# The diagonal block of a bidirectional state-space mixer: both directions in one exponential, step sizes applied by GpSimd to the mask product, one matmul per head

## The chip, the cores and the metric

The kernel runs on one core of a Trainium2 chip. The metric is the device time of one execution in microseconds. The engines are TensorE (PE; its weight loads are listed as PEld), VectorE (DVE), ScalarE (ACT), GpSimd (POOL) and SyncE (SP), each with its own instruction queue; they meet through semaphores.

## What is computed

The layer is an encoder: RMSNorm with modulation, an input projection, two mixers side by side (8 heads of latent attention, 8 heads of a bidirectional Mamba-2 scan), an output projection, then a 16-expert mixture and a last RMSNorm. It runs on a prompt of 512 tokens and a sample of 1024. The change concerns the part of the scan within a chunk of 128 tokens:

```python
cs = jnp.cumsum(dt * a.reshape(g, r), axis=2)
seg = cs[:, :, :, None] - cs[:, :, None, :]
decay_in = jnp.exp(jnp.where(lower, seg, -jnp.inf))
cb = jnp.einsum('bcqgn,bcsgn->bcqsg', cm, bm)
m = cb[..., None] * decay_in * dt[:, :, None]
y_diag = jnp.einsum('bcqsgr,bcsgrp->bcqgrp', m, x)
...
y_fwd = _ssd_scan(xh, dt[:, :, 0], a[0], bm, cm)
y_bwd = flip(_ssd_scan(flip(xh), flip(dt[:, :, 1]), a[1], flip(bm), flip(cm)))
y = y_fwd + y_bwd + d_skip.astype(f32)[:, None] * xh.astype(f32)
```

So for each head there is a 128x128 decay matrix for the forward direction (target at or after source) and one for the backward direction (target at or before source), each times a group's C·B product and a source's step size dt, and both are multiplied with the same x.

## The kernel before, in words

The 1,536 tokens are 12 tiles of 128: tiles 0 to 3 are the prompt, tiles 4 to 11 the sample. The program runs in stages (`inputs`, `attend`, `output`, `choice`, `experts`, `final`). The change is in `attend`, in the function `mixers`, which runs once for the prompt and once for the sample. In it each engine has a body for one tile g that goes through the 8 attention heads h = 0 to 7 (512 keys for the prompt, 1024 for the sample), and work of the scan, of the previous tile's end and of the next tile's query (`front`) is written by hand between the heads. The order on an engine is the order in the code; nothing is scheduled.

For a head, PE makes the scores (L1792) one head ahead, DVE takes their row maximum (`tops`, L1586) and turns it into a bias (L1589), ACT takes the exponential (L1475), PE turns the result in two halves (`turn_p`, L1805), ACT copies the first half (L1536) and DVE the second (L1715), and every second head PE multiplies with the values (L1815). PE's scores two heads on wait for DVE's copy.

The scan's diagonal part of a tile before the change:

- DVE, head 2 of the tile before: `steps` splits the step terms into a high and a low part (L1597, L1599). DVE (`terms`, L1604; head 3 and head 7) and POOL (`terms`, L1424) multiply them with a triangle of ones, DVE for the forward direction and POOL for the backward one: `r_sum`.
- PE (`seg`, L1843) multiplies `r_sum` with a strict triangle, which gives the segment sums of four heads of one direction in bank `b_y`: four rounds p = 0 to 3 (direction and group), two matmuls each, at heads 0 and 1.
- ACT (`seg_exp`, L1501) takes the exponential of each round, 128x512. PE's next round waits for it.
- DVE (`masked`, L1615) multiplies C·B with the two masks, and (`weights`, L1626) each of the four exponentials with that.
- POOL (L1434) makes `xdt`, x times the step sizes for both directions, in one 128x1024 product. It waits until the tile before has used its own.
- PE (`diag`, L1882) multiplies per head and direction: 16 products of 128x128 with 128x64, summed in pairs in `b_y`. It waits for DVE's `take_off` (L1631), and comes at the end of head 3.

DVE also rotates the next tile's query in head 3 (`rope`, L1135 to L1140, six products), for which PE waits at head 4 (`front`, L1782), and normalises the attention output in head 4 (`norm_o`, L1668), ahead of the maximum of head 5. POOL's third product, D times x (L1439), waits for `gate` (L1650) of the tile before. DVE's `add_off` (L1638), `add_skip` (L1643) and `gate` assemble y at heads 4 and 5.

```python
wait_apart(pool, steps_done, g + 1, pool_turns)
wait_apart(pool, seg_mm, g * 4, pool_turns)
```

These two waits open POOL's `terms`; `wait_apart` is a wait on POOL's own queue.

## Time and profile before

| | us |
|---|---|
| median of 3 runs | 3012.91 (3012.7 to 3015.11) |
| the profiled execution, span from first to last instruction | 3010.1 |
| that execution with what lies around the span (by the median of the runs) | 3012.9 |
| the stage with both mixers, from the prompt's first scores to the last tile's end | 362 to 911 |
| one prompt tile in the middle | 32.6 |
| one sample tile in the middle | 45.3 |

The profiled execution has no separate total of its own beside its span; the runs lie about 2.8 us above that span. The rows are of this one execution. In the timeline a line is: start, duration, engine, line of the kernel, operation, output<-input, shape, count, and in brackets how long the engine sat idle before it and what released it.

### The profile page before, as it was taken

To read this page: it belongs to the slowest core of one execution; us is meant where nothing else is said; L and a number is where in the kernel's file an instruction comes from. 1 tells how busy PE (TensorE), PEld (TensorE's weight loads), DVE (VectorE), ACT (ScalarE), POOL (GpSimd) and SP (SyncE) were. 2 spreads that over 40 slices of the span, in tenths; PEclk is the share of its full clock that TensorE was granted. 3 is DMA by queue.
4 is the path that set the end of the run, shared out by engine and by line. 5 is a ranking of instruction groups with operands and counts; after the bars stand their busy time and mean duration, and the time that the engine had idled before them with its cause. 6 is when DMAs were issued, how large, how long until landed. Compare 5 with 4: busy or idle time off the path is not lost. (4 is left out here: it accounts for less than half of the span.)

```text
span 3010.1 us, 50890 instructions
## 1 busy us (share of the span) xinstructions
PE 2784.9 (93%) x17878; PEld 2411.1 (80%) x17878; DVE 2161.3 (72%) x4155; ACT 1529.6 (51%) x2880; POOL 200.8 (7%) x192
## 2 busy tenths in 40 slices
PE   5999688999998966999999999999999999999993
PEld 4999465666666856999999999999999999999992
DVE  3565776666664458788788788778778778778774
ACT  4443454544543324555555555555555556556552
POOL 0000121011100001000000000000000000000001
PEclk8999898999999978999999999999999999999996
DMA  6111310212214336677677677677677777777654
GB/s 258 63 66 57 118 37 30 94 51 101 99 42 177 140 139 210 219 248 252 218 246 248 223 244 243 226 244 242 228 247 238 228 250 239 227 251 239 228 186 178
DMA packets 359719, 547.41 MB, mean 182 GB/s; under 512 B 14784, under 2 KB 287936, under 8 KB 359616
## 3 DMA queue, kind: packets, MB, share of 16 engines
q1 hardware_dynamic: 350720, 514.59, 50.0%
q0 software_dynamic: 8896, 31.46, 4.5%
q8 instruction: 63, 1.03, 0.1%
q14 instruction: 40, 0.33, 0.0%
HBM read 493.51 MB, written 52.49 MB: 181 GB/s over the span
## 5 line engine op out<-in xcount | busy, mean ns | idle before, releaser
L2606 PE MATMUL banks<-rowsT_parts,weights_high 128*128 128x384 f32 x4096 | 1183.9, 361 | 11.0 <-DVE hidden_parts L2535 7.2
L2607 PE MATMUL banks<-rowsT_parts,weights_low 128*128 128x192 f32 x4096 | 1026.0, 250 | 0.0
L2606 PEld LDWEIGHTS banks<-rowsT_parts,weights_high 128*128 128x128 f32 x4096 | 769.7, 188 | 19.9 <-DVE hidden_parts L2535 9.9
L2607 PEld LDWEIGHTS banks<-rowsT_parts,weights_low 128*128 128x128 f32 x4096 | 783.1, 191 | 1.4
L2472 DVE TENSOR_TENSOR weights_low<-keys_or_w_out,weights_high 128x1024 fp32r<-128x1024 f32 x512 | 603.2, 1217 | 1.4 <-ACT weights_high L2412 1.4
L2412 ACT ACTIVATE weights_high<-keys_or_w_out 128x1024 fp32r<-128x1024 f32 x512 | 523.9, 1049 | 39.6 <-PEq L2210 39.6
L2617 PE MATMUL banks<-weights_high,hidden_parts 128*128 128x512 f32 x1536 | 435.7, 392 | 0.0
L2522 DVE TENSOR_TENSOR h_or_keys_or_sums<-banks,h_or_keys_or_sums 128x192 f32<-128x192 f32 x512 | 181.4, 354 | 327.7 <-ACT h_or_keys_or_sums L2438 327.7
L2438 ACT ACTIVATE h_or_keys_or_sums<-banks 128x192 f32<-128x192 f32 x512 | 165.6, 324 | 457.5 <-PE banks L2607 453.5
L2617 PEld LDWEIGHTS banks<-weights_high,hidden_parts 128*128 128x128 f32 x1536 | 283.4, 188 | 69.8
L2617 PE MATMUL banks<-weights_low,hidden_parts 128*128 128x512 f32 (+1 forms) x1024 | 319.4, 393 | 0.0
L2472 DVE TENSOR_TENSOR weights_low<-slab_down,weights_high 128x1024 fp32r<-128x1024 f32 x256 | 311.4, 1216 | 0.0
L2412 ACT ACTIVATE weights_high<-slab_down 128x1024 fp32r<-128x1024 f32 x256 | 264.3, 1051 | 5.3 <-PE banks L2617 4.9
L2617 PEld LDWEIGHTS banks<-weights_low,hidden_parts 128*128 128x128 f32 (+1 forms) x1024 | 164.9, 161 | 55.8
L2446 ACT ACTIVATE silu_gate<-h_or_keys_or_sums 128x192 f32<-128x192 f32 x256 | 92.5, 361 | 228.3 <-DVE h_or_keys_or_sums L2522 228.3
L1792 PE MATMUL banks<-keys_or_w_out,arena_attend 96*128 96x512 f32 x320 | 159.2, 606 | 6.2 <-DVE arena_attend L1715 4.3
L2385 POOL DMA_INDIRECT residual<-weighted,rows_out x32 | 49.8, 1556 | 1675.5 <-DVE weighted L2511 1675.5
L1536 ACT ACTIVATE arena_attend<-banks 128x512 f32<-128x512 f32 (+1 forms) x96 | 50.5, 526 | 187.8 <-PE banks L1805 187.7
L1586 DVE TENSOR_REDUCE mix_top<-banks 128x1 f32<-128x1024 f32 (+1 forms) x96 | 100.1, 1043 | 42.4 <-PE banks L1792 42.1
L2163 PE MATMUL banks<-w_out_high,mixed_parts 128*128 128x512 f32 x384 | 125.2, 397 | 2.1 <-DVE mixed_parts L2126 1.6
L1805 PEld LDWEIGHTS banks<-masks,arena_attend 128*128 128x128 f32 x640 | 75.6, 142 | 56.2 <-issue 31.9
L995 PE MATMUL banks<-w_in_high,h_parts 128*128 128x512 f32 (+1 forms) x384 | 116.5, 380 | 0.0
(303 smaller groups left out, 3528.7 us busy)
## 6 DMA issues: line engine op xcount, KB each, us to landing
keys_or_w_out<-w_gate SPq DMA_DIRECT2D x128, 1024.0 KB, 5.1
keys_or_w_out<-w_up SPq DMA_DIRECT2D x128, 1024.0 KB, 6.8
slab_down<-w_down SPq DMA_DIRECT2D x128, 1024.0 KB, 4.8
arena_attend<-w_ada SPq DMA_DIRECT2D x8, 2048.0 KB, 7.6
arena_attend<-ssd_tiles SPq DMA_DIRECT2D x12, 992.0 KB, 9.0
arena_inputs<-w_ada SPq DMA_DIRECT2D x4, 2048.0 KB, 11.4
ssd_tiles<-arena_inputs SPq DMA_DIRECT2D x24, 256.0 KB, 2.0
mixed<-arena_attend SPq DMA_DIRECT2D x12, 512.0 KB, 3.3
```

The costliest lines, as they stand in the source:

```text
L995: mm = nc.tensor.matmul(out, a, b, start=(k == 0 and n == 0), stop=(k == KD - 1 and n == 2))
L1586: nc.vector.tensor_reduce(top[:, h % 2:h % 2 + 1], core.banks[:, h % 2 * 1024:h % 2 * 1024 + keys_n], AX_X, ALU.max).then_inc(topped, 1)
L1792: mm = nc.tensor.matmul(core.banks[:, h % 2 * 1024 + k0:h % 2 * 1024 + k0 + 512], qT[j][0:DQK, h, :], kT[0:DQK, h, k0:k0 + 512], start=Tru ...
L2163: mm = nc.tensor.matmul(core.ps[6 * j + half], a, b[:, k, cols], start=(k + n == 0), stop=(k == 7 and n == 2))
L2412: nc.scalar.activation(like(n, w_hi), unit_of(raw, n), ACT.Copy).then_inc(unit_hi, 1)
L2438: nc.scalar.activation(sums[:, kind, fc % 2], core.ps[2 * (fc % 2) + kind][:, CT:2 * CT], ACT.Copy).then_inc(low_out, 1)
L2446: nc.scalar.activation(sil[:, fc % 2], sums[:, 0, fc % 2], ACT.Silu).then_inc(sil_done, 1)
L2472: nc.vector.tensor_tensor(like(n, w_lo), unit_of(raw, n), like(n, w_hi[:].bitcast(F32)), ALU.subtract).then_inc(unit_lo, 1)
L2522: nc.vector.tensor_tensor(sums[:, kind, fc % 2], core.ps[2 * (fc % 2) + kind][:, 0:CT], sums[:, kind, fc % 2], ALU.add).then_inc(sum_done, 1)
L2606: nc.tensor.matmul(out[:, 0:2 * CT], w_hi[:, u, block], x[:, k, :], start=k == 0, stop=False)
L2607: mm = nc.tensor.matmul(out[:, 0:CT], w_lo[:, u, block], x[:, k, 0:CT], start=False, stop=k == KD - 1)
L2617: mm = nc.tensor.matmul(y_banks[b][0:rows, cols], h_parts[:, fc, tokens], w[:, u, cols], start=step == 0 and first, stop=step == STEPS - 1 ...
```

## The change

Since a strict triangle gives zero outside its direction's half, the segment sums of both directions can be added into one bank: each of the two rounds now has four matmuls (two directions, two parts) and gives four heads of both directions. One exponential per round follows, so two of 128x512 per tile in place of four. The masks move into a new product of POOL, `cb_times_dt`: mask times step sizes for each direction (two of 128x1024), their sum (128x1024), and that times C·B (two of 128x512). DVE multiplies the two exponentials with it (`weights`), and `masked` keeps only its two copies. `diag` is one product per head on x itself: 8 in place of 16. POOL's `xdt` is gone. The tile `cbdt` takes the room of `e`'s second half, and `xdt` and `cbm` are no longer there.

```diff
             def terms(g, j):
...
-                wait_apart(pool, seg_mm, g * 4, pool_turns)
+                wait_apart(pool, seg_mm, g * 2, pool_turns)
...
+            def cb_times_dt(g, j):
+
+                wait_apart(pool, m_done, g * 2, pool_turns)
+                for d, (out, m) in enumerate(((cbdt, M_LE), (cbdt_b, M_GE))):
+                    nc.gpsimd.tensor_tensor(out, core.masks[:, m, :].unsqueeze(1).broadcast_to([P, NS, P]),
+                                            dt[j][:, 8 * d:8 * d + 8].unsqueeze(2).broadcast_to([P, NS, P]),
+                                            ALU.mult).then_inc(cbdt_order, 1)
+                wait_apart(pool, cbdt_order, g * 3 + 2, pool_turns)
+                nc.gpsimd.tensor_tensor(cbdt, cbdt, cbdt_b, ALU.add).then_inc(cbdt_order, 1)
+                wait_apart(pool, cbdt_order, g * 3 + 3, pool_turns)
+                for grp in range(2):
+                    part = cbdt[:, 4 * grp:4 * grp + 4, :]
+                    ins = nc.gpsimd.tensor_tensor(part, part, cb[j][:, P * grp:P * grp + P].unsqueeze(1).broadcast_to([P, 4, P]),
+                                                  ALU.mult)
+                ins.then_inc(cbdt_done, 1)
...
             def first():
                 if not r:
                     terms(lo, 0)
+                    cb_times_dt(lo, 0)
...
-                wait_apart(pool, diag_mm, g, pool_turns)
-                nc.gpsimd.tensor_tensor(xdt, heads(xnat[j]).unsqueeze(1).broadcast_to([P, 2, NS, HP]),
...
                 if after(i, more)[0]:
                     terms(g + 1, 1 - j)
+                    cb_times_dt(g + 1, 1 - j)
...
-            def seg_exp(g, p):
+            def seg_exp(g, grp):
...
-                nc.scalar.activation(e[:, p // 2, 4 * (p % 2):4 * (p % 2) + 4, :], b_y.rearrange("p (h q) -> p h q", h=4),
+                nc.scalar.activation(e[:, 4 * grp:4 * grp + 4, :], b_y.rearrange("p (h q) -> p h q", h=4),
...
-                for d in range(2):
-                    nc.vector.tensor_tensor(cbm[:, d], cb[j].rearrange("p (a q) -> p a q", a=2),
...
+            def weights(g, grp):
+
+                if grp == 0:
+                    dve.wait_ge(cbdt_done, g + 1)
+                dve.wait_ge(e_done, g * 2 + (grp + 1))
+                part = e[:, 4 * grp:4 * grp + 4, :]
+                nc.vector.tensor_tensor(part, part, cbdt[:, 4 * grp:4 * grp + 4, :], ALU.mult).then_inc(m_done, 1)
...
                     if h in (1, 2):
-                        weights(g, 2 * h - 2)
+                        weights(g, h - 1)
...
-                    if h in (1, 2):
-                        weights(g, 2 * h - 1)
...
+                for d in range(2):
+                    for part in range(2):
+                        mm = nc.tensor.matmul(b_y, turns_r[:, d, :],
+                                              r_sum[:, part, d, 4 * grp:4 * grp + 4, :].rearrange("p h q -> p (h q)"),
+                                              start=d + part == 0, stop=d + part == 2)
...
                 for h in range(NS):
-                    for d in range(2):
-                        mm = nc.tensor.matmul(b_y[:, h * HP:(h + 1) * HP], e[:, d, h, :], xdt[:, d, h, :],
-                                              start=(d == 0), stop=(d == 1))
+                    mm = nc.tensor.matmul(b_y[:, h * HP:(h + 1) * HP], e[:, h, :], xnat[j][:, h * HP:(h + 1) * HP],
+                                          start=True, stop=True)
```

The order on the engines moves at three places. The first is POOL, one tile, around one tile's `terms` (L1424; L1434 is `xdt`, L1439 D times x). Before:

```order
L1434 TENSOR_TENSOR arena_attend<-arena_attend 128x1024
L1439 TENSOR_TENSOR arena_attend<-arena_attend,rows 128x512
L1424 TENSOR_TENSOR decay_steps<-masks,steps_high 128x1024
L1424 TENSOR_TENSOR decay_steps<-masks,steps_low 128x1024
L1434 TENSOR_TENSOR arena_attend<-arena_attend 128x1024
```

With the change (L1423 is `terms`; L1431, L1435 and L1439 are `cb_times_dt`; L1450 is D times x):

```order
L1450 TENSOR_TENSOR arena_attend<-arena_attend,rows 128x512
L1423 TENSOR_TENSOR decay_steps<-masks,steps_high 128x1024
L1423 TENSOR_TENSOR decay_steps<-masks,steps_low 128x1024
L1431 TENSOR_TENSOR arena_attend<-masks,arena_attend 128x1024 x2
L1435 TENSOR_TENSOR arena_attend<-arena_attend 128x1024
L1439 TENSOR_TENSOR arena_attend<-arena_attend 128x512 x2
```

POOL's block behind `terms` has five instructions where it had one, and they stand in the same run as `terms`, where `xdt` came after the wait for `diag`.

The second is DVE, prompt tile 0, head 2 into head 3: the second copy of `turn_p`, the scan's steps, and the maximum of head 4. Before:

```order
L1586 TENSOR_REDUCE mix_top<-banks 128x1
L1589 TENSOR_SCALAR mix_bias<-mix_top 128x1
L1715 COPY arena_attend<-banks 128x256
L1626 TENSOR_TENSOR arena_attend<-arena_attend 128x512
L1597 CAST steps_high<-arena_attend 128x16
L1599 TENSOR_TENSOR steps_low<-arena_attend,steps_high 128x16
L1631 TENSOR_TENSOR arena_attend<-banks,arena_attend 128x512
L1586 TENSOR_REDUCE mix_top<-banks 128x1
```

With the change:

```order
L1596 TENSOR_REDUCE mix_top<-banks 128x1
L1599 TENSOR_SCALAR mix_bias<-mix_top 128x1
L1719 COPY arena_attend<-banks 128x256
L1607 CAST steps_high<-arena_attend 128x16
L1609 TENSOR_TENSOR steps_low<-arena_attend,steps_high 128x16
L1635 TENSOR_TENSOR arena_attend<-banks,arena_attend 128x512
L1596 TENSOR_REDUCE mix_top<-banks 128x1
```

The product `weights` (L1626 before) between the copy and `steps` (L1597, now L1607) is gone, so `steps`, which POOL waits for, comes one product earlier.

The third is PE, prompt tile 0, from the state's first product (L1858, now L1861) to the values of head 4. Before:

```order
L1858 MATMUL banks<-arena_attend,c_groups 128x256 x2
L1792 MATMUL banks<-keys_or_w_out,arena_attend 128x512
L1805 MATMUL banks<-masks,arena_attend 128x128 x2
L1858 MATMUL banks<-arena_attend,c_groups 128x256 x2
L1805 MATMUL banks<-masks,arena_attend 128x128 x2
L1882 MATMUL banks<-arena_attend 128x64 x16
L1792 MATMUL banks<-keys_or_w_out,arena_attend 128x512
L1815 MATMUL banks<-arena_attend 64x128 x8
```

With the change:

```order
L1861 MATMUL banks<-arena_attend,c_groups 128x256 x2
L1794 MATMUL banks<-keys_or_w_out,arena_attend 128x512
L1807 MATMUL banks<-masks,arena_attend 128x128 x2
L1861 MATMUL banks<-arena_attend,c_groups 128x256 x2
L1807 MATMUL banks<-masks,arena_attend 128x128 x2
L1883 MATMUL banks<-arena_attend 128x64 x8
L1794 MATMUL banks<-keys_or_w_out,arena_attend 128x512
L1817 MATMUL banks<-arena_attend 64x128 x8
```

Nothing moves here but the count of the diagonal's products: 16 before, 8 now, at the same place.

## Rows read from the trace of the kernel before

**Rows 1.** The page, busy time of each engine: us (share of the span) xinstructions

```profile
PE 2784.9 (93%) x17878; PEld 2411.1 (80%) x17878; DVE 2161.3 (72%) x4155; ACT 1529.6 (51%) x2880; POOL 200.8 (7%) x192
```

**Rows 2.** Windows of one tile each: PE, PEld, DVE, ACT, POOL busy (x), PEclk, DMA

```profile
402.70:435.30 32.60, 29.23 (x191) 20.51 (x190) 26.37 (x56) 16.57 (x47) 6.73 (x4) 0.96 0.01 5
635.80:681.10 45.30, 44.12 (x369) 31.15 (x368) 31.15 (x58) 22.09 (x50) 6.70 (x4) 1.00 0.22 83
```

**Rows 3.** Timeline, PE, sample tile: start us, us, engine line op, names, shapes [idle before]

```profile
656.76 3.76 PE L1882 MATMUL banks<-arena_attend 128*128 128x64 f32 x32 [0.45 <-DVE arena_attend L1631]
660.35 1.94 PE L1792 MATMUL banks<-keys_or_w_out,arena_attend 96*128 96x512 f32 x4
```

**Rows 4.** Lines, ACT exponentials and DVE weights: duration ns min/median/max

```profile
L1501 ACT ACTIVATE arena_attend<-banks x48: 587/597/626, 371.6 to 872.0; 128x512 f32<-128x512 f32 x48
L1626 DVE TENSOR_TENSOR arena_attend<-arena_attend x48: 679/682/685, 373.0 to 877.1; 128x512 f32<-128x512 f32 x48
```

**Rows 5.** Timeline, POOL, same sample tile

```profile
653.95 1.90 POOL L1424 TENSOR_TENSOR decay_steps<-masks,steps_high 128x1024 fp32r<-128x1024 f32 x1 [25.88 <-DVE steps_low L1599]
655.81 1.90 POOL L1424 TENSOR_TENSOR decay_steps<-masks,steps_low 128x1024 fp32r<-128x1024 f32 x1
660.70 1.90 POOL L1434 TENSOR_TENSOR arena_attend<-arena_attend 128x1024 f32<-128x1024 f32 x1 [2.99 <-PE banks L1882]
```

**Rows 6.** Timeline, DVE and POOL, first prompt tile

```profile
362.37 1.23 DVE L1604 TENSOR_TENSOR decay_steps<-masks,steps_high 128x1024 fp32r<-128x1024 f32 x1
362.71 2.65 POOL L1424 TENSOR_TENSOR decay_steps<-masks,steps_high 128x1024 fp32r<-128x1024 f32 x1 [362.12 <-DVE steps_low L1599]
363.52 2.92 DVE L1604 TENSOR_TENSOR decay_steps<-masks,steps_low 128x1024 fp32r<-128x1024 f32 x1
365.32 2.87 POOL L1424 TENSOR_TENSOR decay_steps<-masks,steps_low 128x1024 fp32r<-128x1024 f32 x1
366.36 1.98 DVE L1570 TENSOR_SCALAR arena_attend<-h_or_keys_or_sums,mix_q_rstd 128x256 f32<-128x256 f32 x1
368.15 1.94 POOL L1434 TENSOR_TENSOR arena_attend<-arena_attend 128x1024 f32<-128x1024 f32 x1
370.06 1.04 POOL L1439 TENSOR_TENSOR arena_attend<-arena_attend,rows 128x512 f32<-128x512 f32 x1
```

**Rows 7.** Timeline, DVE, same sample tile, heads 3 and 4

```profile
655.93 0.68 DVE L1631 TENSOR_TENSOR arena_attend<-banks,arena_attend 128x512 f32<-128x512 f32 x1
657.13 0.73 DVE L1135 TENSOR_TENSOR arena_attend<-arena_attend,rope 128x128 f32<-128x128 f32 x1
658.91 1.22 DVE L1604 TENSOR_TENSOR decay_steps<-masks,steps_high 128x1024 fp32r<-128x1024 f32 x1
660.04 0.48 DVE L1668 TENSOR_SCALAR arena_attend<-arena_attend,mix_o_rstd 128x512 f32<-128x512 f32 x1
662.32 1.23 DVE L1586 TENSOR_REDUCE mix_top<-banks 128x1 f32<-128x1024 f32 x1 [1.80 <-PE banks L1792]
```

**Rows 8.** Timeline, DVE and PE, same sample tile, what follows

```profile
664.61 0.60 PE L1782 MATMUL banks<-masks,arena_attend 128*96 128x128 f32 x4
668.21 1.22 DVE L1586 TENSOR_REDUCE mix_top<-banks 128x1 f32<-128x1024 f32 x1
669.56 0.69 DVE L1715 COPY arena_attend<-banks 128x512 f32<-128x512 f32 x1
670.30 1.13 PE L1792 MATMUL banks<-keys_or_w_out,arena_attend 96*128 96x512 f32 x2 [0.58 <-DVE arena_attend L1715]
```

**Rows 9.** Timeline, DVE, first prompt tile, heads 3 to 5

```profile
385.17 1.74 DVE L1135 TENSOR_TENSOR arena_attend<-arena_attend,rope 128x128 f32<-128x128 f32 x1
389.77 0.69 DVE L1586 TENSOR_REDUCE mix_top<-banks 128x1 f32<-128x512 f32 x1 [0.60 <-PE banks L1792]
394.08 0.68 DVE L1586 TENSOR_REDUCE mix_top<-banks 128x1 f32<-128x512 f32 x1
```

**Rows 10.** Timeline, DVE, first prompt tile, first weights product

```profile
373.01 0.68 DVE L1626 TENSOR_TENSOR arena_attend<-arena_attend 128x512 f32<-128x512 f32 x1
```

More of the change, by code:

```diff
@@ L1127 @@
 A_QT, A_O = 28800, 30848
-A_E, A_XDT, A_Y, A_CBM = 32896, 34944, 35968, 38016
+A_E, A_CBDT, A_Y = 32896, 33920, 35968
 A_REC, A_JUNKM = 38528, 24064
@@ L1291, in mixers @@
     step_lo = core.once("steps_low", [P, 2, 16])
-    e = A.at(A_E, 2, NS, P)
-    xdt = A.at(A_XDT, 2, NS, HP)
+    e = A.at(A_E, NS, P)
+    cbdt, cbdt_b = A.at(A_CBDT, NS, P), A.at(A_CBDT + 1024, NS, P)
     y = A.at(A_Y, 4, DSSD)
-    cbm = A.at(A_CBM, 2, 2, P)
     ctz = core.once("c_groups", [P, 2, P])
@@ L1311, in mixers @@
     act_order, o_order, rope_order, inv_done = sem("q_act_order"), sem("att_o_order"), sem("att_rope_order"), sem("att_inv")
-    terms_f, terms_b, seg_mm, e_done, m_done, cbm_done, ctz_done, xdt_done, xd_done = (
-        sem(n) for n in ("terms_f", "terms_b", "seg_mm", "seg_exp", "m_done", "cbm_done", "c_groups", "xdt_done", "xd_done"))
+    terms_f, terms_b, seg_mm, e_done, m_done, cbdt_done, ctz_done, cbdt_order, xd_done = (
+        sem(n) for n in ("terms_f", "terms_b", "seg_mm", "seg_exp", "m_done", "cb_dt", "c_groups", "cb_dt_order", "xd_done"))
     off_mm, off_done, diag_mm, y_order, gated, y_sq, s_rstd_done, y_normed, y_turned, y_mixed = (
@@ L1539, in body @@
                     if h < 2:
-                        seg_exp(g, 2 * h)
+                        seg_exp(g, h)
                     if h + 1 < NH:
@@ L1613, in masked @@
                 nc.vector.tensor_copy(ctz[64:128, 1, :], ct[j][64:128, :]).then_inc(ctz_done, 1)
-                for d in range(2):
-                    nc.vector.tensor_tensor(cbm[:, d], cb[j].rearrange("p (a q) -> p a q", a=2),
-                                            core.masks[:, (M_LE, M_GE)[d], :].unsqueeze(1).broadcast_to([P, 2, P]),
-                                            ALU.mult).then_inc(cbm_done, 1)
-            def weights(g, p):
-                d, grp = divmod(p, 2)
-                if p == 0:
-                    dve.wait_ge(cbm_done, g * 2 + 2)
-                dve.wait_ge(e_done, g * 4 + (p + 1))
-                part = e[:, d, 4 * grp:4 * grp + 4, :]
-                nc.vector.tensor_tensor(part, part, cbm[:, d, grp:grp + 1, :].broadcast_to([P, 4, P]),
-                                        ALU.mult).then_inc(m_done, 1)
+            def weights(g, grp):
+                if grp == 0:
+                    dve.wait_ge(cbdt_done, g + 1)
+                dve.wait_ge(e_done, g * 2 + (grp + 1))
+                part = e[:, 4 * grp:4 * grp + 4, :]
+                nc.vector.tensor_tensor(part, part, cbdt[:, 4 * grp:4 * grp + 4, :], ALU.mult).then_inc(m_done, 1)
             def take_off(g, j, d):
@@ L1696, in body @@
                     if h == 0:
-                        masked(g, j)
+                        c_groups(g, j)
                     if before and h == 1:
@@ L1832, in turn_o, with seg @@
                 mm.then_inc(o_turned, 1)
-            def seg(g, p, behind):
-                d, grp = divmod(p, 2)
-                pe.wait_ge((terms_f, terms_b)[d], g + 1 if d else g * 2 + 2)
-                if p:
-                    pe.wait_ge(e_done, g * 4 + p)
+            def seg(g, grp, behind):
+                pe.wait_ge(terms_f, g * 2 + 2)
+                pe.wait_ge(terms_b, g + 1)
+                if grp:
+                    pe.wait_ge(e_done, g * 2 + 1)
                 elif behind is not None:
                     pe.wait_ge(y_mixed, behind + 1)
-                for part in range(2):
-                    mm = nc.tensor.matmul(b_y, turns_r[:, d, :],
-                                          r_sum[:, part, d, 4 * grp:4 * grp + 4, :].rearrange("p h q -> p (h q)"),
-                                          start=part == 0, stop=part == 1)
+                for d in range(2):
[3 more added lines that the diff above has]
+                                              start=d + part == 0, stop=d + part == 2)
                 mm.then_inc(seg_mm, 1)
@@ L1850, in off @@
                 if d == 0:
-                    pe.wait_ge(e_done, g * 4 + 4)
+                    pe.wait_ge(e_done, g * 2 + 2)
                     pe.wait_ge(ctz_done, g + 1)
@@ L1918, in body @@
                     if h < 2:
-                        seg(g, 2 * h, g - 1 if before or r else None)
+                        seg(g, h, g - 1 if before or r else None)
                     if h == 3:
@@ L1931, in body @@
                     if h == 3:
-                        diag(g)
+                        diag(g, j)
                     if before and h == 6:
```

18 lines of the change are left out of this document (5 added, 13 removed).

## The prediction

> **What bounds the kernel now.** I read the page's busy times first [rows 1]: PE 93%, DVE 72%, POOL 7% over the whole span. These are averages over stages, and the change touches one of them, so the next view was the windows of single tiles in that stage [rows 2]. A sample tile lasts 45.3 us, with PE busy 44.1 of them, DVE 31.2 and POOL 6.7: there PE is the bound. A prompt tile lasts 32.6 us, with PE at 29.2 and DVE at 26.4: there neither is full, and the time is a chain that goes scores, maximum, exponential, turn, copy from engine to engine. The chain that ended last lies wholly in the final stage and says nothing of this one. So for each part I ask two things: what it takes off PE in a sample tile, and what it does to the time at which DVE delivers the maximum of a head, on which both kinds of tile hang. The third view was the timeline of one sample tile and of the first prompt tile. A measurement of this kernel can tell about 0.2%, some 6 us, from no change.
>
> **PE.** The diagonal's 16 products are 32 passes, and the next matmul starts 3.6 us after the first of them (656.76 to 660.35) [rows 3]. Half of them gone is 1.8 us per tile if PE is the bound, 21.6 us over 12 tiles. The segment sums keep their eight matmuls, and only stand in two runs of four. The first exponential waits for two matmuls more, the second comes later than the second did; I take that at nothing, since ACT is idle for half of a sample tile [rows 2]. If ACT were full it would cost the two matmuls, under 1 us.
>
> **ACT and DVE, work removed.** ACT loses two exponentials of 0.60 us and DVE two products of 0.68 us [rows 4], and DVE also loses the two mask products, which are half as wide. That is 1.2 us on ACT and about 2 us on DVE per tile, all at heads 0 to 2. In a sample tile PE covers them (DVE has 14 us free), so nothing. In a prompt tile the exponential of the next head stands behind the scan's on ACT, so a little may come through: between 0 and 2 us, and I take 0.5 us, because one of the two exponentials that stay now waits for its later matmuls.
>
> **POOL.** It loses `xdt`, 1.9 us, and gains three products of 128x1024 and two of 128x512. The nearest rows for these are 1.90 us for L1424 and 1.04 us for the 128x512 product at 370.06 [rows 5, 6]. Laid end to end, started every 1.86 us as the first two are, that is about 7.7 us, so POOL goes from 6.7 to 12.6 us of a 45.3 us tile. The result is needed only at head 1 of the next tile, over 10 us after it is done. By busy time this is free, and in the steady tiles no wait on the result itself will show.
>
> **Where it is not free.** The timeline of the first prompt tile has DVE and POOL side by side [rows 6]. A DVE product of 1.22 us starts at 362.37; POOL's, issued at 362.71, takes 2.65 us, that is 1.90 after the DVE product has ended. The DVE product at 363.52 takes 2.92: it ends 1.1 us after POOL's first has ended at 365.36. POOL's second (365.32) takes 2.87 and ends 1.9 us after that. The DVE scaling at 366.36 takes 1.98 us and ends 0.15 us after POOL is done. So of these instructions only one runs at a time, and at each release the one that has waited goes, so they take turns. Not every DVE instruction is concerned: at 655.93 one that reads PSUM and SBUF runs in its usual 0.68 us in the middle of POOL's second product, while the first rotation product at 657.13 takes 0.73 us and ends just after that product (657.71) [rows 5, 7]. In the prompt the same one takes 1.74 us [rows 9].
>
> The change puts five more POOL instructions exactly there. `steps` comes 0.6 us earlier (one DVE product less ahead of it), so POOL's `terms` run from 653.3 to 657.1 and `cb_times_dt` follows at once, where before POOL was silent from 657.7 to 660.7 [rows 5]. DVE then has eight instructions of the kind that waits: six rotation products, its own `terms` and `norm_o`, which took from 657.71 to 660.52 together, 2.8 us [rows 7]. If each POOL instruction gets its turn among the eight, DVE is through at 657.1 + 7.7 + 2.8 = 667.6 us. POOL waits for its own results twice inside the block, and in such a gap a DVE instruction may slip in; then up to two of the five fall behind DVE's eight, and it is through at 665.6. I take the middle, 666.6.
>
> Queued behind these on DVE is the maximum of head 5, which started at 662.32 after 1.80 us of idling for PE [rows 7]. It starts 4.3 us later. From it to the maximum of head 6, without waiting, are 1.35 us (the maximum and its bias) and the 2.5 us of the four instructions between 665.68 and 668.21: 3.9 us, so 670.5 in place of 668.21; the copy of head 5 follows 1.35 us later, and 0.74 us after its start PE can begin the second half of scores 7 [rows 8]. That is 672.6 in place of 670.30: **a sample tile gets 2.3 us longer** (1.3 to 3.3), and PE's 1.8 us are lost in this wait, since the diagonal lies ahead of it. PE will also stand at the turn of the rotated query (664.61 before [rows 8]). Seven sample tiles have a next one: 7 x 2.3 = 16 us. The last has none, and keeps its 1.8 us.
>
> In a prompt tile POOL's `terms` end at 386.2, and DVE is through at 386.2 + 7.7 + 2.4 = 396.3, or 2 earlier; middle 395.3. The maximum of head 5 was at 389.77 and that of head 6 at 394.08 [rows 9], 3.1 us behind it when DVE does not wait: 398.4, 4.3 us later. Less the 0.5 us above and rounded, **a prompt tile gets 4 us longer** (3 to 5): 16 us over four.
>
> At the very start POOL's block stands before the first tile's `weights`. POOL is done with `terms` at 368.2, and with the block near 376.2, where `weights` ran at 373.01 [rows 10]: 3.2 us late, of which DVE's waiting for PE hides a part; I take 2 (1 to 3.2).
>
> The Trainium skill (SBUF — State Buffer, the section on the two separate sides) calls the pair of ports that DVE and GpSimd share an exclusive lock, held for a whole instruction, against DVE instructions with two SBUF inputs or in a 2-port mode. It does not say who is next when it comes free. If DVE kept it over its eight instructions it would wait once, 1.9 us, be through at 657.1 + 1.9 + 2.8 = 661.8, before the maximum can start, and the sum would be the gain of rival one below; rows 6 show turns instead.
>
> **Sum.** 16 + 16 + 2 - 1.8 = 32 us on the profiled span of 3010.1 us, plus the 2.8 us by which the median of the runs (3012.9) lies above it: 3045 us. With the terms' lower bounds it is 20 us (3033), with the upper ones 45 us (3058).
>
> **Rivals.** One: the DVE instructions get through (they wait once, or PE's slack at heads 4 to 6 covers them), and the removed matmuls count. For it: DVE is idle 14 us of a sample tile, and 1.8 us of that stands right before the maximum of head 5. Then 1.8 us x 8 in the sample, and 0 to 1.8 x 4 in the prompt: 14 to 22 us faster, 2991 to 2999 us. It decides if DVE's eight instructions are delayed by less than about 1.8 us; the four alternations of rows 6 speak against it. Two: half of the turns slip by, and wait and gain cancel: 3007 to 3019. Three: the waits also lower the clock. The granted clock was 1.00 in the sample tile and 0.96 in the prompt one, where PE is less busy [rows 2], so new idle stretches may send a part of each tile to the lower of the two levels (1.2 of 2.4 GHz). At 0.96 in the sample's seven tiles, some 4% of 45.3 us each, that is 12 us more: 3057 or above.
>
> **How the numbers follow.** The forecast has 0.62, rival three 0.14, both slower; rival two 0.06, no change; rival one 0.18, faster. The time is that of the forecast, 3045. The range goes from 3004 to 3066: it leaves out rival one (0.18) and little above. The forecast's own range is 3033 to 3058.
>
> **What would show it.** Right: the six rotation products and DVE's `terms`, 2.9 us busy in a sample tile without waiting, together take over 5 us longer; POOL's five products directly behind `terms`; PE idle at heads 4 to 6 for DVE's maximum, copy or rotation, while its diagonal takes 1.8 us; sample tiles of 47 to 49 us, prompt tiles of 35.5 to 37.5. Wrong: sample tiles of 43.5 us with rotation products of 0.28 us, or a loss at heads 0 to 2, which this text takes as nothing.

## The result and the profile after

The changed kernel takes 3063.1 us (median of 4 runs, 3058.81 to 3063.99) against 3013.1 us, a ratio of 1.016 (95% interval 1.0148 to 1.0172): 50 us slower, where 32 were forecast. Its profiled execution has a span of 3062.2 us, 52.1 more than before, and a time of 3063.9 us.

The page's busy times of the kernel after, which answer to [rows 1]:

```profile
PE 2791.5 (91%) x17686; PEld 2403.2 (78%) x17686; DVE 2214.4 (72%) x4107; ACT 1518.2 (50%) x2856; POOL 287.0 (9%) x240
```

PE has 192 passes fewer (96 products of the diagonal, two passes each), and POOL is busy for 287 us in place of 201. Windows of one prompt tile and two sample tiles of the kernel after (busy of PE, PEld, DVE, ACT, POOL; granted clock of TensorE; DMA share; GB/s), against [rows 2]:

```profile
421.40:458.70 37.30, 29.88 (x175) 19.72 (x174) 30.35 (x53) 16.08 (x48) 14.47 (x8) 0.86 0.13 46
677.90:729.10 51.20, 46.62 (x352) 31.34 (x351) 36.53 (x55) 21.30 (x48) 13.63 (x8) 0.90 0.20 75
829.20:878.00 48.80, 44.32 (x352) 30.17 (x351) 36.27 (x55) 21.30 (x48) 13.65 (x9) 0.97 0.20 75
```

A sample tile takes 48.8 or 51.2 us where it took 45.3, a prompt tile 37.3 where it took 32.6. POOL is busy for 13.6 us of a sample tile where 12.6 were forecast: its sum of two whole tensors (L1435) takes 2.35 to 2.39 us in each of the twelve tiles, where I had put the 1.90 of L1424, and a product with C·B (L1439) at least 1.26 us, where I had put 1.04. It is not DVE that makes them that long; rows of e2 below show it. DVE is busy for 36.5 or 36.3 us, five more than before, though it has fewer instructions: it is booked as busy while it waits for POOL. The granted clock is 0.97 and 0.90 where it was 1.00.

Where the 52 us lie, by marks that both timelines have (the first product of POOL's `terms` for a tile, the first matmul of a stage):

| stretch | before, us | after, us | difference |
|---|---|---|---|
| start to tile 0's `terms` | 362.7 | 364.8 | 2.0 |
| to tile 1's | 20.3 | 21.0 | 0.7 |
| to tile 4's (three prompt tiles) | 100.7 | 110.5 | 9.8 |
| to tile 5's (last of the prompt, sample keys) | 79.9 | 82.6 | 2.7 |
| to tile 11's (six sample tiles) | 271.5 | 299.2 | 27.7 |
| to the output projection | 91.9 | 93.5 | 1.6 |
| to the experts | 232.9 | 233.1 | 0.2 |
| experts, first to last gate product | 1785.9 | 1792.6 | 6.7 |
| the rest | 64.3 | 65.0 | 0.7 |

The mixers hold 42.5 us, and 6.7 lie in the expert stage, of which no line was changed. Start and rest scatter by about as much between the kernels below.

The cause in a sample tile, first on DVE and POOL. Timeline of the kernel after, DVE, heads 3 and 4 of the tile at 678 (compare [rows 7]; L1596 is the maximum of head 5):

```profile
681.68 1.98 DVE L1135 TENSOR_TENSOR arena_attend<-arena_attend,rope 128x128 f32<-128x128 f32 x1
683.58 1.98 DVE L1136 TENSOR_TENSOR arena_attend<-arena_attend,rope 128x128 f32<-128x128 f32 x1
685.49 0.28 DVE L1137 TENSOR_TENSOR arena_attend<-arena_attend,rope 128x128 f32<-128x128 f32 x1
685.69 2.44 DVE L1138 TENSOR_TENSOR arena_attend<-arena_attend,rope 128x128 f32<-128x128 f32 x1
688.16 0.29 DVE L1139 TENSOR_TENSOR arena_attend<-arena_attend 128x128 f32<-128x128 f32 x1
688.37 1.35 DVE L1140 TENSOR_TENSOR arena_attend<-arena_attend 128x128 f32<-128x128 f32 x1
689.64 2.29 DVE L1614 TENSOR_TENSOR decay_steps<-masks,steps_high 128x1024 fp32r<-128x1024 f32 x1
691.85 0.47 DVE L1672 TENSOR_SCALAR arena_attend<-arena_attend,mix_o_rstd 128x512 f32<-128x512 f32 x1
692.25 1.21 DVE L1596 TENSOR_REDUCE mix_top<-banks 128x1 f32<-128x1024 f32 x1
```

And POOL in the same stretch (compare [rows 5]):

```profile
679.76 1.90 POOL L1423 TENSOR_TENSOR decay_steps<-masks,steps_low 128x1024 fp32r<-128x1024 f32 x1
681.62 3.80 POOL L1431 TENSOR_TENSOR arena_attend<-masks,arena_attend 128x1024 f32<-128x1024 f32 x2
685.59 2.38 POOL L1435 TENSOR_TENSOR arena_attend<-arena_attend 128x1024 f32<-128x1024 f32 x1 [0.18 <-POOL arena_attend L1431]
688.15 2.69 POOL L1439 TENSOR_TENSOR arena_attend<-arena_attend 128x512 f32<-128x512 f32 x2 [0.18 <-POOL arena_attend L1435]
```

The first rotation product waits for POOL's first mask product (to 683.5), the second for the next (to 685.4), the third slips into the 0.18 us in which POOL waits for its own result, the fourth waits for the sum, the fifth slips in again, the sixth waits for one product with C·B, and DVE's `terms` for the last. The eight instructions last from 681.68 to 692.3 in place of 657.13 to 660.5. The maximum behind them takes 1.21 us as ever, but POOL is done by then (690.84); that a maximum, which reads PSUM, is not slowed beside a POOL product is shown by e1 below.

Then on PE, the same stretch (compare [rows 3, 8]; L1883 is the diagonal, L1784 the turn of the rotated query, L1794 the scores):

```profile
681.31 1.97 PE L1883 MATMUL banks<-arena_attend 128*128 128x64 f32 x16 [0.45 <-DVE arena_attend L1635]
683.12 1.94 PE L1794 MATMUL banks<-keys_or_w_out,arena_attend 96*128 96x512 f32 x4
689.77 0.64 PE L1784 MATMUL banks<-masks,arena_attend 128*96 128x128 f32 x4 [2.24 <-DVE arena_attend L1140]
694.34 2.07 PE L1794 MATMUL banks<-keys_or_w_out,arena_attend 96*128 96x512 f32 x2 [1.74 <-DVE arena_attend L1719]
696.21 1.06 PE L1807 MATMUL banks<-masks,arena_attend 128*128 128x128 f32 x4
```

The diagonal takes 1.8 us in place of 3.6 (683.12 less 681.31). After it PE stands 2.24 us for the sixth rotation product and 1.74 us for DVE's copy of head 4, which is queued behind the maximum of head 5. The last row shows a third loss: four turn passes (x4) take 1.06 us where the same four take 0.60 elsewhere in the tile, so PE runs at the lower of its two clock levels (1.2 of 2.4 GHz). It does so from about 690.7, between the two waits, to 700.9, some 10 of the tile's 51.2 us, which is what the window's 0.90 says.

### The profile page after: what moved, and what is told of

Same layout as the page of the kernel before. It is cut to its first block and busy times, and to the rows that moved or that the text cites. A ratio compares the mean times of both kernels' runs of the same rounds, so it can differ in the third digit from the quotient of the medians.

```text
span 3062.2 us, 50465 instructions
## 1 busy us (share of the span) xinstructions
PE 2791.5 (91%) x17686; PEld 2403.2 (78%) x17686; DVE 2214.4 (72%) x4107; ACT 1518.2 (50%) x2856; POOL 287.0 (9%) x240
## 5 line engine op out<-in xcount | busy, mean ns | idle before, releaser
L2445 ACT ACTIVATE silu_gate<-h_or_keys_or_sums 128x192 f32<-128x192 f32 x256 | 92.6, 362 | 232.9 <-DVE h_or_keys_or_sums L2521 232.9
L1794 PE MATMUL banks<-keys_or_w_out,arena_attend 96*128 96x512 f32 x320 | 176.6, 662 | 14.9 <-DVE arena_attend L1719 13.0
L1487 ACT ACTIVATE arena_attend<-banks,mix_bias 128x1024 f32<-128x1024 f32 (+1 forms) x96 | 93.1, 970 | 93.7 <-DVE mix_bias L1599 93.6
L1596 DVE TENSOR_REDUCE mix_top<-banks 128x1 f32<-128x1024 f32 (+1 forms) x96 | 100.2, 1043 | 33.9 <-PE banks L1794 33.3
```

The source lines that it names most:

```text
L1487: nc.scalar.activation(prob[h % 2][:, 0:keys_n], core.banks[:, h % 2 * 1024:h % 2 * 1024 + keys_n], ACT.Exp, bias=bias[:, h % 2:h % 2 + 1] ...
L1596: nc.vector.tensor_reduce(top[:, h % 2:h % 2 + 1], core.banks[:, h % 2 * 1024:h % 2 * 1024 + keys_n], AX_X, ALU.max).then_inc(topped, 1)
L1794: mm = nc.tensor.matmul(core.banks[:, h % 2 * 1024 + k0:h % 2 * 1024 + k0 + 512], qT[j][0:DQK, h, :], kT[0:DQK, h, k0:k0 + 512], start=Tru ...
L2445: nc.scalar.activation(sil[:, fc % 2], sums[:, 0, fc % 2], ACT.Silu).then_inc(sil_done, 1)
```

## Experiments

The two theories: DVE and GpSimd take turns at something that both need, so five long POOL instructions behind `terms` hold up DVE's eight and through them PE; or the new order at heads 0 to 2 (a run of four matmuls, two exponentials, the wait for POOL's product) costs the time. In the table a ratio is to the kernel before on the same chip; "tile" is the distance of two tiles' `terms` in the profiled execution, in the prompt between tiles 2 and 3 and in the sample between tiles 8 and 9.

| kernel | median us | ratio (95%) | prompt tile | sample tile | experts |
|---|---|---|---|---|---|
| before | 3013.1 | | 32.6 | 45.3 | 1785.9 |
| the change | 3063.1 | 1.0160 (1.0148 to 1.0172) | 37.3 | 51.2 | 1792.6 |
| e1 block moved | 3007.6 | 0.9985 (0.9976 to 0.9995) | 33.7 | 43.7 | 1792.1 |
| e2 block small | 2995.5 | 0.9945 (0.9926 to 0.9965) | 29.7 | 43.7 | 1792.1 |
| e3 block in 16 | 3027.3 | 1.0042 (1.0026 to 1.0059) | 34.5 | 45.3 | 1792.3 |
| e4 before plus block | 3053.8 | 1.0131 (1.0114 to 1.0148) | 39.7 | 47.9 | 1786.0 |
| e5 change, diagonal twice | 3061.9 | 1.0157 (1.0141 to 1.0172) | 36.9 | 48.9 | 1792.3 |
| e6 moved, diagonal twice | 3031.4 | 1.0058 (1.0043 to 1.0074) | 35.5 | 45.5 | 1792.5 |
| e7 moved, padded | 3003.5 | 0.9967 (0.9955 to 0.9979) | 33.7 | 43.7 | 1786.7 |
| e8 moved, padded, in 16 | 2997.7 | 0.9946 (0.9932 to 0.9960) | 31.7 | 43.7 | 1786.3 |
| e9 before, padded by 3 | 3013.9 | 0.9999 (0.9990 to 1.0007) | 32.6 | 45.3 | 1785.9 |
| e10 change, padded | 3058.2 | 1.0143 (1.0128 to 1.0158) | 37.3 | 48.8 | 1786.6 |
| e11 as e8, tile 0 in long products | 2994.8 | 0.9934 (0.9921 to 0.9946) | 31.7 | 43.7 | 1786.1 |

The change's six sample tiles are 49.5, 49.7, 51.2, 51.2, 48.9 and 48.8 us; e10's, which has the same mixers, lie between 48.5 and 50.7, and e3's between 44.9 and 46.9. The longest tiles of each are those with its lowest granted clock (0.90 in the change and e10, 0.96 in e3).

**e1: the block at another place.**

```diff
             def first():
                 if not r:
                     terms(lo, 0)
-                    cb_times_dt(lo, 0)
...
                 wait_apart(pool, gated, g, pool_turns)
+                cb_times_dt(g, j)
...
                     terms(g + 1, 1 - j)
-                    cb_times_dt(g + 1, 1 - j)
```

> The change with cb_times_dt taken from behind terms to the wait for the tile before's gate (head 5), ahead of D times x; nothing else differs. Turn-taking theory: at heads 6 and 7 DVE has fewer instructions of the kind that waits (gate, norm_y, terms' second part, two copies) and more room, so rope products fall back to 0.3 to 0.7 us, PE keeps its 1.8 us per sample tile, the clock is 1.00 there: sample tiles of 43.5 to 45 us, 2992 to 3010 us in all. Rival, that the new order at heads 0 to 2 (four matmuls in a run, two exponentials, the wait for POOL's product) costs the time: stays at 3055 to 3065.

Measured: 3007.6 us. Everything that the change does is still done, and only the place of POOL's block differs, so the new order at heads 0 to 2 is not what costs. Windows of this kernel, one prompt and one sample tile:

```profile
418.70:452.40 33.70, 28.19 (x175) 18.44 (x174) 28.23 (x53) 16.37 (x48) 14.28 (x9) 0.95 0.15 51
697.50:741.20 43.70, 42.51 (x352) 29.29 (x351) 30.95 (x55) 21.21 (x48) 14.48 (x8) 1.00 0.23 87
```

The sample tile is 1.6 us shorter than before the change and PE is busy for all but 1.2 us of it; the clock is 1.00 again. The prompt tile is still 1.1 us longer than before. Its timeline shows why: at the new place DVE's second part of `terms` and its two copies wait. DVE, e1:

```profile
470.08 3.04 DVE L1613 TENSOR_TENSOR decay_steps<-masks,steps_low 128x1024 fp32r<-128x1024 f32 x1
474.31 1.31 DVE L1621 COPY c_groups<-arena_attend 64x128 f32<-64x128 f32 x1
475.63 0.99 DVE L1622 COPY c_groups<-arena_attend 64x128 f32<-64x128 f32 x1
```

They take 1.22, 0.21 and 0.22 us without company. The maximum does not wait. DVE and POOL of e1, in a sample tile:

```profile
718.94 1.22 DVE L1595 TENSOR_REDUCE mix_top<-banks 128x1 f32<-128x1024 f32 x1 [1.47 <-PE banks L1793]
718.83 2.36 POOL L1435 TENSOR_TENSOR arena_attend<-arena_attend 128x1024 f32<-128x1024 f32 x1 [0.18 <-POOL arena_attend L1431]
```

**e2: the block small.**

```diff
-            def cb_times_dt(g, j):
+            def cb_times_dt(g, j, n=8):
...
-                    nc.gpsimd.tensor_tensor(out, core.masks[:, m, :].unsqueeze(1).broadcast_to([P, NS, P]),
+                    nc.gpsimd.tensor_tensor(out[:, :, 0:n], core.masks[:, m, 0:n].unsqueeze(1).broadcast_to([P, NS, n]),
```

> The change with cb_times_dt in full for tile 0 only; from tile 1 its five instructions at the same place cover 8 of 128 columns each (the other columns keep tile 0's values: the mask product of all later tiles is left out but for these). Turn-taking theory: the five hold the ports for some 0.1 to 0.2 us each, rope is as before, 2990 to 3003 us. Rival, heads 0 to 2: 3055 to 3065. Rival, that the number of POOL instructions counts and not their length: over 3040.

Measured: 2995.5 us. The number of POOL instructions and all waits are those of the change, only their length is gone, and with it 68 us. This is also what the rest of the change is worth: its windows

```profile
414.05:443.73 29.68, 26.39 (x175) 17.64 (x174) 23.13 (x53) 16.18 (x48) 7.22 (x8) 1.00 0.16 57
681.10:724.80 43.70, 42.51 (x352) 29.29 (x351) 29.28 (x55) 21.19 (x48) 6.36 (x8) 1.00 0.24 87
```

have 43.7 us for a sample tile and 29.7 for a prompt tile, 2.9 less than before. I had expected half a microsecond from the lighter heads 0 to 2 and nothing from the diagonal; the 2.9 us hold both, and the runs do not part them here (the diagonal's part is 1.8 us in e6 against e1). With 6.2 us in the expert stage taken off, an estimate from the table, it would be at 2989.

In e2's first tile, where the block is in full, DVE reads PSUM or has one short instruction beside the sum, and stands idle beside the two products with C·B. POOL, e2:

```profile
372.82 2.35 POOL L1435 TENSOR_TENSOR arena_attend<-arena_attend 128x1024 f32<-128x1024 f32 x1 [0.18 <-POOL arena_attend L1431]
375.35 2.52 POOL L1439 TENSOR_TENSOR arena_attend<-arena_attend 128x512 f32<-128x512 f32 x2 [0.18 <-POOL arena_attend L1435]
```

So 2.35 and 1.26 us are what these instructions take by themselves.

**e3: the same work in shorter instructions.**

```diff
-                    nc.gpsimd.tensor_tensor(out, core.masks[:, m, :].unsqueeze(1).broadcast_to([P, NS, P]),
-                                            dt[j][:, 8 * d:8 * d + 8].unsqueeze(2).broadcast_to([P, NS, P]),
-                                            ALU.mult).then_inc(cbdt_order, 1)
+                    for q in range(0, NS, 2):
+                        ins = nc.gpsimd.tensor_tensor(out[:, q:q + 2, :], core.masks[:, m, :].unsqueeze(1).broadcast_to([P, 2, P]),
+                                                      dt[j][:, 8 * d + q:8 * d + q + 2].unsqueeze(2).broadcast_to([P, 2, P]),
+                                                      ALU.mult)
```

(and so for the sum and the products with C·B)

> The change with the same products at the same place, in 16 POOL instructions of 128x256 instead of three of 128x1024 and two of 128x512. By the two shapes seen (1.04 and 1.90 us) one should take 0.6 us, the block 9.8 us in place of 7.7. Turn-taking theory: each of DVE's eight instructions waits for one of 0.6 us, under 5 us in place of 7.7, so sample tiles of 46 to 48 us and prompt tiles shorter by 2 to 3 us: 3025 to 3045 us. Rival, that DVE loses what POOL works in all, whoever's turn it is: 2 us more per tile than the change, 3075 to 3090.

Measured: 3027.3 us, 36 us less than the change, at the same place and with more work on POOL. The rows are the plainest of the study. DVE, e3:

```profile
758.90 0.69 DVE L1135 TENSOR_TENSOR arena_attend<-arena_attend,rope 128x128 f32<-128x128 f32 x1
759.52 0.70 DVE L1136 TENSOR_TENSOR arena_attend<-arena_attend,rope 128x128 f32<-128x128 f32 x1
760.14 0.70 DVE L1137 TENSOR_TENSOR arena_attend<-arena_attend,rope 128x128 f32<-128x128 f32 x1
760.75 0.70 DVE L1138 TENSOR_TENSOR arena_attend<-arena_attend,rope 128x128 f32<-128x128 f32 x1
761.49 0.59 DVE L1139 TENSOR_TENSOR arena_attend<-arena_attend 128x128 f32<-128x128 f32 x1
762.00 0.69 DVE L1140 TENSOR_TENSOR arena_attend<-arena_attend 128x128 f32<-128x128 f32 x1
762.62 1.63 DVE L1618 TENSOR_TENSOR decay_steps<-masks,steps_high 128x1024 fp32r<-128x1024 f32 x1
764.17 0.84 DVE L1676 TENSOR_SCALAR arena_attend<-arena_attend,mix_o_rstd 128x512 f32<-128x512 f32 x1
```

POOL, e3:

```profile
758.83 5.89 POOL L1432 TENSOR_TENSOR arena_attend<-masks,arena_attend 128x256 f32<-128x256 f32 x8
764.90 3.26 POOL L1438 TENSOR_TENSOR arena_attend<-arena_attend 128x256 f32<-128x256 f32 x4 [0.18 <-POOL arena_attend L1432]
```

Each rotation product takes 0.6 to 0.7 us in place of 0.28: each waits for exactly one POOL product of 128x256. POOL's eight products take 5.89 us, 0.74 each, since it waits for DVE's as well. That is turns, one instruction each; a loss in proportion to POOL's work would have made this kernel the slowest.

**e4: the block alone, in the kernel before.** It writes to room that nothing reads, and POOL waits for itself four times in it where the change's block waits twice, because both mask products share that room.

```diff
+            def block(g, j):
+                order = xdt_done
+                wait_apart(pool, order, g * 5 - 4, pool_turns)
+                for d, m in enumerate((M_LE, M_GE)):
+                    if d:
+                        wait_apart(pool, order, g * 5 - 3, pool_turns)
+                    nc.gpsimd.tensor_tensor(spare, core.masks[:, m, :].unsqueeze(1).broadcast_to([P, NS, P]),
...
                 if after(i, more)[0]:
                     terms(g + 1, 1 - j)
+                    block(g + 1, 1 - j)
```

> The kernel before, with a block of five POOL products of the same shapes as cb_times_dt behind terms, written to room that nothing reads (one more wait of POOL on itself than in the change); nothing is removed. Turn-taking theory: the waits come without any of the change's other parts: sample tiles of 49 to 52 us, 3055 to 3080 us. Rival, heads 0 to 2 of the change: no effect, 3012 to 3018.

Measured: 3053.8 us, 41 us over before, by the block alone. DVE, e4:

```profile
684.89 1.98 DVE L1136 TENSOR_TENSOR arena_attend<-arena_attend,rope 128x128 f32<-128x128 f32 x1
687.00 1.98 DVE L1138 TENSOR_TENSOR arena_attend<-arena_attend,rope 128x128 f32<-128x128 f32 x1
689.22 1.98 DVE L1140 TENSOR_TENSOR arena_attend<-arena_attend 128x128 f32<-128x128 f32 x1
```

Every second rotation product waits for a long one. The window of one sample tile of e4:

```profile
728.96:776.84 47.88, 44.19 (x368) 31.16 (x367) 37.55 (x59) 22.18 (x49) 16.16 (x9) 1.00 0.21 79
```

47.9 us at a clock of 1.00, as in its other sample tiles (47.5 to 47.9). Time and tile lie a little below what I had expected (3055 us and 49). Its waits are not quite the change's: it has 16 diagonal products, starts POOL 0.6 us later and has more gaps in its block, and the maximum of head 5 starts 9.4 us after the first rotation product where it starts 10.6 after it in the change. PE does not stand at the rotated query, and stands for the copies of heads 4 and 5 for 2.13 and 0.95 us. So e4 shows that the block alone costs the time, but not what the clock's part is in the change; e5 and e10 do.

**e5 and e6: the diagonal's products made twice.**

```diff
                 for h in range(NS):
-                    mm = nc.tensor.matmul(b_y[:, h * HP:(h + 1) * HP], e[:, h, :], xnat[j][:, h * HP:(h + 1) * HP],
-                                          start=True, stop=True)
+                    for d in range(2):
+                        mm = nc.tensor.matmul(b_y[:, h * HP:(h + 1) * HP], e[:, h, :], xnat[j][:, h * HP:(h + 1) * HP],
+                                              start=(d == 0), stop=(d == 1))
```

> The change with the diagonal's product of each head made twice into the same place (16 products of 128x64 instead of 8, so the diagonal term is doubled). Theory: in the change the 1.8 us that PE saves are lost in its wait for the rotation and for the copy of head 4 that stand behind DVE's eight instructions, so giving them back costs nothing: within 3 us of the change, 3058 to 3066, and more PE work may even hold the clock up. Rival, that the saving counts in full: 14 to 22 us above the change, 3077 to 3085.

> The same doubling on the version with cb_times_dt moved to the gate of the tile before (3007.6 us). There PE is the bound of a sample tile again, so eight more products cost 1.8 us in each of the eight sample tiles and some of it in the prompt: 3022 to 3029 us. Rival, that PE's saving is never on the path: 3005 to 3011.

Measured: 3061.9 us on the change (3063.1), 3031.4 us on the moved version (3007.6). On the change eight more products per tile cost nothing: the saving is lost in the waits behind it, as foreseen. On the moved version they cost 24 us, 2 more than the upper end of what I had put. PE in e5, at the same two places as above:

```profile
739.01 0.64 PE L1784 MATMUL banks<-masks,arena_attend 128*96 128x128 f32 x4 [1.56 <-DVE arena_attend L1140]
742.50 1.12 PE L1794 MATMUL banks<-keys_or_w_out,arena_attend 96*128 96x512 f32 x2 [1.55 <-DVE arena_attend L1719]
```

It stands 1.56 and 1.55 us there, and 0.58 us for the next copy, as before the change. And one sample tile each of e5 and e6:

```profile
726.00:774.90 48.90, 44.61 (x368) 31.05 (x367) 36.47 (x55) 21.35 (x48) 13.46 (x8) 1.00 0.21 78
```

```profile
712.44:757.94 45.50, 44.31 (x368) 31.08 (x367) 30.99 (x55) 21.22 (x48) 14.50 (x8) 1.00 0.22 84
```

e6's tile is 1.8 us longer than e1's (45.5 and 43.7), PE bound. In the prompt 1.8 us come through too in the tiles after 1 and 2, and 5.0 in the one after 3, whose clock is 0.87 where e1's is 0.95.

e5's tile is 48.9 us long at a clock of 1.00, and so are all but one of its six (48.5 to 48.9; the other 51.0 at 0.93). Of e10's six, in which the mixers are the change's, one holds the clock. Its window, and PE's first two waits in it (L1786 is the turn of the rotated query, L1796 the scores):

```profile
728.25:777.08 48.83, 42.80 (x352) 29.26 (x351) 36.40 (x55) 21.31 (x48) 13.62 (x8) 1.00 0.21 78
740.12 0.64 PE L1786 MATMUL banks<-masks,arena_attend 128*96 128x128 f32 x4 [2.22 <-DVE arena_attend L1140]
744.68 1.13 PE L1796 MATMUL banks<-keys_or_w_out,arena_attend 96*128 96x512 f32 x2 [2.62 <-DVE arena_attend L1719]
```

So the waits alone make a sample tile 3.5 us longer, and the clock adds between nothing and 2.4 us. In the change's six tiles, 299.2 us in sum, that is an estimate of 21 us for the waits (six of 48.8 us are 292.8, against 271.5 before) and 6 us for the clock.

**e7, e9, e10: the expert stage.** The change's program has 45 instructions less on DVE ahead of the expert loop (waits included). In all kernels made from the one before, DVE pauses 0.23 us before its weighting, in the unpadded ones made from the change 0.55 us (3.5 and 8.3 us over 15 turns; the expectations have 0.24 and 0.58, which leave the first turn out). PE's wait for DVE's `hidden_parts` in that stage grows with it, from 7.2 to 13.0 us, which is most of the 6.7; it is 7.1 us in e7, e9 and e10. From the waits of DVE (total us, times, longest), the change, then e7, then e9:

```profile
DVE weighted L2510 <- DVE weighted L2507: 8.3, 15, 0.6
```

```profile
DVE weighted L2511 <- DVE weighted L2508: 3.5, 15, 0.3
```

```profile
DVE weighted L2513 <- DVE weighted L2510: 3.5, 15, 0.3
```

The edit of e7 and e10; e9 has 3 in place of 45, on the kernel before:

```diff
             def last(g, j):
                 if r:
+                    for i in range(45):
+                        nc.vector.memset(A.at(38016 + i, 1), 0.0)
                     divide(g, j)
```

> The moved version with 45 DVE memsets of one column put before the last tile's divide, where DVE waits for PE anyway, so that the program of DVE in the expert stage stands at the same distance from its start as before the change (the change made it 45 instructions shorter). Theory, that the pause of DVE before its weighting in the expert loop, 0.24 us in the kernels made from the one before and 0.58 us in those made from the change, is a matter of where the code lies: the expert stage goes from 1792 back to 1786 us, 3000 to 3003 us in all. Rival, that it is data or memory placement: stays at 1792, 3007 to 3011 us.

> The change itself with the 45 memsets: the expert stage back at 1786 us, the mixers as in the change: 3055 to 3059 us. Rival, that the expert stage's 6.7 us come from what the mixers left behind: 3060 to 3065.

> The kernel before with three DVE memsets of one column ahead of the last tile's divide, so that its expert loop stands where it does in the change but for a multiple of 16 instructions (the change is 45 shorter, this one 3 longer). Theory, code placement within blocks of instructions: DVE's pause before the weighting goes from 0.24 to 0.58 us and the expert stage from 1786 to 1792 us: 3018 to 3021 us. Rival, that only the same distance from the start counts, or something else in the change: 3012 to 3015.

Measured: 3003.5, 3058.2 and 3013.9 us. e7 and e10 have the expert stage at 1786.7 and 1786.6 us and the short pause, e9 has them too (1785.9). So the 6.7 us are no matter of what the mixers left: 45 small DVE instructions ahead of the loop take them away, with the mixers as they are in the change. But my rule of a multiple of 16 fell with e9: 3 more change nothing. That it is the place of the code is a reading that no run here shows, and by which rule it would act stays open.

**e8 and e11: a version that beats both.** e8 joins e1, e3 and the padding; e11 makes tile 0's block of the five long products.

```diff
+                w = NS if isinstance(g, int) and g == 0 else 2
+                v = min(w, 4)
...
-                    for q in range(0, NS, 2):
+                    for q in range(0, NS, w):
```

> The padded moved version with cb_times_dt in 16 products of 128x256. In the moved version's prompt tiles (33.7 us) DVE's two norm products, terms' second part and two copies still wait for POOL's long products; turn-taking theory: short ones cut these waits by half, prompt tiles of 31 to 32.5 us, 2994 to 3000 us. Rival, that the total of POOL's work counts: prompt tiles of 34 us or more.

> The moved, split and padded version (2997.7 us) with tile 0's cb_times_dt in the five long products again, since nothing hides that block and 16 short products take some 2 us more than five long ones: the first tile takes 21 us in place of 24, 2993 to 2996 us. Rival, that the first tile waits for something else: no change, 2996 to 2999.

Measured: 2997.7 and 2994.8 us. The prompt tile falls from 33.7 to 31.7 us, within the bounds; e11's first tile takes 20.95 us where e8's took 24.05. One prompt tile of e11:

```profile
418.56:450.23 31.67, 28.02 (x175) 18.54 (x174) 25.12 (x53) 16.21 (x48) 16.16 (x19) 0.95 0.15 54
```

It is 2 us above e2's 29.7, which is what the block still costs there; a part of it is the clock, 0.95 against e2's 1.00. e11 is 0.66% faster than the kernel before.

## Why the prediction was right, and where its sizes were off

**The mechanism** was the forecast's. Turns at the release, POOL's block in the same run as `terms`, PE standing at the rotated query and at DVE's copy, the 1.8 us of the diagonal lost in that wait (e5), nothing lost at heads 0 to 2 (e1): all as written. The rival that ends faster fails on the change itself, and e3 and e4 show why; it is what the change would be without the block's length (e2) or with the block elsewhere.

**Sum, first term: the sample tiles, 14 us forecast (16 less 1.8), 29 measured** (27.7 and 1.6). Two sizes were short.

The first is the wait. The delay of the maximum of head 5 was taken in the middle, 4.3 us, of bounds of 3.3 and 5.3; from the first rotation product to that maximum it is 10.6 us after (681.68 to 692.25) and 5.2 before, 5.4 later. The allowance for slipping by did not come true: two rotation products went into POOL's two gaps, but the others still waited for all five of POOL's. And the block lasts 9.2 us (681.62 to 690.84) where I had laid end to end 7.7, by rows of products in which one operand is a single number for 64 or more columns; that the upper bound is met all the same, and not passed by 1.5, is because DVE's rotation products add nearly nothing to POOL's block (its two mask products take 3.80 us with one of them between), and I had counted them in full. The chain from there was the forecast's: in the tile at 829 that maximum, the next one, its copy and the second half of scores 7 start at 843.54, 847.42, 848.77 and 849.51, that is 3.9, 1.35 and 0.74 us apart. PE has a wait one head earlier too, for the copy of head 4, but it does not end last. With the clock at 1.00 a tile is 3.5 us longer (e10), where 2.3 were forecast (1.3 to 3.3).

The second is the clock, some 6 us over the six tiles. It is rival three, given 0.14, priced at 12 us and held apart from the forecast; it was not another case but followed from this one. It cost less than its price because a slow stretch that lies ahead of a wait of PE costs nothing: the tile at 829 has a clock of 0.97 and is no longer than e10's at 1.00.

**Second term: the prompt, 16 us and 2 at the start, 13.2 measured** (9.8 and 2.7, and 0.7 at the start). Both parts of it were too small. Over the three prompt tiles that the table of stretches takes together, e4's block costs 17.1 us, 5.7 per tile (117.7 against 100.7), where the delay was put at 4.3. And e5, which has the change's block and as many diagonal products as e4, takes 111.1 us for the same three, 2.2 per tile less than e4: so much is all that parts the two worth, which I read as the lighter heads 0 to 2 in the main, where I had put 0.5. No run shows that part alone.

**What was missing: 6.7 us in the experts**, which 45 DVE instructions ahead of them take away. No row of the profile before could have shown it.

So 32 us against the 52 of the profiled execution (50 by the medians) is 15 too few in the sample, 5 too many in the prompt, 6.7 for the experts, and about 3 in stretches that scatter. The time lies above the forecast's own range of 3033 to 3058 and where rival three was to lie; that it is not further off is in part luck, since the prompt's error goes the other way.

## What to carry to other kernels

Work put on an idle GpSimd is not free because GpSimd is idle: look at which VectorE instructions run at that moment, and if they work on SBUF alone (products, scalings and copies did, here), count one whole GpSimd instruction for each until one side runs out, save for those that slip into a gap in which GpSimd waits for itself. Put such a block where VectorE reads PSUM or waits, and cut it into short instructions if it can't be moved; both are edits of a few lines, worth 55 and 36 us here. Where a wait is added behind which PE stands, look also for a fall of its clock.

## What the runs showed of the hardware

- DVE and GpSimd alternate instruction by instruction: with GpSimd products of 128x1024 (1.90 us) the rotation product takes 1.98 us in place of 0.28, with ones of 128x256 it takes 0.70 (e3). DVE instructions that read PSUM ran at their usual 0.68 us (`take_off`, rows 7) and 1.22 us (e1's maximum at 718.94) beside them. The Trainium skill (SBUF — State Buffer, the section on the two separate sides) describes a lock that is held for a whole instruction, and the traces agree with it: 1.98 us behind products of 1.90, and 0.70 in e3.
- A gap of 0.18 us, in which GpSimd waits for its own result, can let one DVE instruction through (685.49 in the kernel after, 0.28 us).
- A GpSimd instruction of 128x1024 on fp32 took 1.90 to 1.94 us as a product in which one operand is a single number for 128 columns (L1431), and 2.35 to 2.39 us as the sum of two whole tensors (L1435); in 128x256 it is 0.61 and 0.71 us at the least (e8).
- PE's clock fell to the lower level for 3 to 10 us in each of the change's six sample tiles; in the tiles at 678 and 829 that began behind a wait of PE of 2.2 us, or at its end. It did not in a tile of e10, the same mixers, with waits of 2.22 and 2.62 us, nor in five of e5's six, with eight more products and 1.56 and 1.55 us. So the length of the waits alone does not tell whether it falls.
- In the kernels with 45 DVE instructions less ahead of a loop a pause in it was 0.32 us longer per turn, and the stage 6 to 7 us; 45 memsets brought both back, and three more than in the kernel before did nothing.
